# Score banks, mask products and the split of a residual in a two-block hybrid network

## The reference, cut to what matters

```
z = rmsnorm(x) @ w_in                     # cut into four mixers of 4 heads x 64
o_a = retention(q, k, v)                  # scores (k q^T) * decay, times v
o_b = gated_delta(q, k, v, beta, g)       # needs the inverse of (1 + beta * kk)
o_c, o_d = gated_linear(q, k, v, log_f)   # scores with a decay per channel
x  = x + concat(norm(o) * gates) @ w_out            # product "mix_out"
x  = x + attn(rmsnorm(x) * att_norm, mem) @ wo      # product "att_o"
x  = x + conv_ffn(rmsnorm(x) * ffn_norm)            # begins with product "up_0"
```

## Time and profile before

| | |
|---|---|
| median of the runs | 2508.35 us |
| the profiled execution | 2508.84 us, span 2507.0 us |
| PE busy | 2406.8 us, 96% of the span |
| DVE busy | 1731.7 us, 69% |
| ACT busy | 677.4 us, 27% |
| POOL busy | 196.8 us, 8% |
| granted clock of TensorE over the span | 0.98 |

### The profile page before, as it was taken

One profiled execution on the slowest core, in us unless ns is written; L12 is line 12 of the kernel. 1 busy time (PEld: TensorE's weight loads), 2 busy tenths in 40 slices (PEclk: granted clock), 3 DMA queues, 4 the chain that ended last, 5 costly groups with the idle time before them and its releaser, 6 DMA issues. The chain is left out here.

```text
span 2507.0 us, 34255 instructions
## 1 busy us (share of the span) xinstructions
PE 2406.8 (96%) x13948; PEld 1951.7 (78%) x13948; DVE 1731.7 (69%) x2700; ACT 677.4 (27%) x1248; POOL 196.8 (8%) x169
## 2 busy tenths in 40 slices
PE   8997879999999999999999999999999999999997
PEld 6885768887788888787765578888888888888886
DVE  7663666866888875738878777666666886666653
ACT  3212444012111110423577712222202112322200
POOL 0001341100000002000121010000010001000001
PEclk9998989999999999999999999999999999999999
DMA  5220002331233354422210073323463452223341
GB/s 186 76 74 0 3 19 76 111 118 51 84 96 98 97 186 146 152 68 76 76 35 1 2 247 98 109 93 101 149 239 107 160 214 72 93 93 101 122 143 63
DMA packets 70333, 252.82 MB, mean 101 GB/s; under 512 B 7808, under 2 KB 8096, under 8 KB 69664
## 3 DMA queue, kind: packets, MB, share of 16 engines
q1 hardware_dynamic: 69888, 250.08, 29.9%
q10 hardware_dynamic: 288, 0.54, 0.1%
HBM read 248.50 MB, written 2.10 MB: 100 GB/s over the span
## 5 line engine op out<-in xcount | busy, mean ns | idle before, releaser
L393 PE MATMUL psum<-rounded_n,rounded_high 128*128 128x512 f32 x1856 | 737.9, 398 | 4.4 <-DVE rounded_n_low L547 1.8
L395 PE MATMUL psum<-rounded_n,rounded_ring 128*128 128x512 f32 x1856 | 725.3, 391 | 0.0
L394 PE MATMUL psum<-rounded_n_low,rounded_high 128*128 128x512 f32 x1856 | 725.1, 391 | 0.0
L347 DVE TENSOR_TENSOR rounded_ring<-ring,rounded_high 128x1024 fp32r<-128x1024 f32 (+1 forms) x360 | 446.4, 1240 | 43.4 <-ACT rounded_high L330 31.4
L393 PEld LDWEIGHTS psum<-rounded_n,rounded_high 128*128 128x128 f32 x1856 | 350.4, 189 | 84.9 <-issue 7.5
L394 PEld LDWEIGHTS psum<-rounded_n_low,rounded_high 128*128 128x128 f32 x1856 | 350.4, 189 | 77.4 <-issue 5.5
L395 PEld LDWEIGHTS psum<-rounded_n,rounded_ring 128*128 128x128 f32 x1856 | 350.0, 189 | 73.7
L345 DVE CAST rounded_high<-ring 128x1024 fp32r<-128x1024 f32 (+1 forms) x347 | 236.6, 682 | 189.1 <-PE psum L395 182.2
L393 PE MATMUL psum<-rounded_arena,rounded_high 128*128 128x512 f32 x720 | 280.9, 390 | 4.4 <-DVE rounded_ring L347 4.4
L394 PE MATMUL psum<-rounded_arena,rounded_high 128*128 128x512 f32 x720 | 280.6, 390 | 0.0
L395 PE MATMUL psum<-rounded_arena,rounded_ring 128*128 128x512 f32 x720 | 280.6, 390 | 0.0
(11 more groups left out here) (478 smaller groups left out, 3030.4 us busy)
## 6 DMA issues: line engine op xcount, KB each, us to landing
ring<-in_w_up SPq DMA_DIRECT2D x132, 512.0 KB, 3.5
ring<-in_w_down SPq DMA_DIRECT2D x48, 512.0 KB, 3.5
n_low<-in_mod_w SPq DMA_DIRECT2D x48, 512.0 KB, 5.6
arena<-in_mod_w SPq DMA_DIRECT2D x48, 512.0 KB, 5.4
ring<-in_w_ab_in SPq DMA_DIRECT2D x37, 512.0 KB, 3.5
ring<-in_w_mix_in SPq DMA_DIRECT2D x31, 512.0 KB, 3.5
ring<-in_w_sc_in SPq DMA_DIRECT2D x24, 512.0 KB, 5.4
ring<-in_w_down SPq DMA_DIRECT2D x24, 384.0 KB, 3.1
```

The costliest lines, as they stand in the source:

```text
L347: nc.vector.tensor_tensor(self.rounded(raw), raw, self.rounded(high), ALU.subtract).then_inc(self.weights_split, 1)
L393: self.nc.tensor.matmul(out, w_high, x_high, start=first, stop=False)
L394: self.nc.tensor.matmul(out, w_high, x_low, start=False, stop=False)
L395: return self.nc.tensor.matmul(out, w_low, x_high, start=False, stop=last)
```

## The change

It consists of five edits in two functions.

1. Retention's scores alternate between two pairs of banks, G0 and G0+1 for even steps and D0+2 and D0+3 for odd ones. The wait of `ret_scores(i)` is for the weighting of step i - 2. Step 1 waits for all weighting of the delta mixer, which reads D0 to D0+3.
2. In PE's queue scores stand two steps ahead of values.
3. `first_inverse(2)` and `(3)`, which write banks D0+2 and D0+3, follow behind the last values on PE.
4. On POOL each pick stands one turn earlier: pick HEADS+x+3 ahead of the decayed keys of turn x.
5. In a residual product with a gain ACT writes the high part n from h and the gain in one activation, ahead of its square. DVE writes the low part as gain times h minus that high part in one instruction. The memory's two low parts stand ahead of it.

```diff
+    RET_BANK = (G0, D0 + 2)
...
             if i == 0:
                 pe.wait_ge(taken, TURNS)
+            elif i == 1:
+                pe.wait_ge(weighted, 2 * HEADS)
             else:
-                pe.wait_ge(ret_weighted, 2 * i)
+                pe.wait_ge(ret_weighted, 2 * i - 2)
...
         ret_scores(0)
+        ret_scores(1)
         for i in range(RETS):
             ret_values(i)
-            if i + 1 < RETS:
-                ret_scores(i + 1)
-            if i >= 2 and i % 2 == 0:
+            if i + 2 < RETS:
+                ret_scores(i + 2)
+            if i in (2, 4):
                 first_inverse(i // 2 - 1)
+        first_inverse(2)
         first_inverse(3)
...
         pick(HEADS + 1)
+        pick(HEADS + 2)
         for x in range(len(uses)):
             u, s = uses[x]
-            if HEADS + x + 2 < HEADS * len(LEVELS):
-                pick(HEADS + x + 2)
+            if HEADS + x + 3 < HEADS * len(LEVELS):
+                pick(HEADS + x + 3)
...
+            if gain is not None:
+                nc.scalar.activation(k.rounded(k.n[:, j, :]), k.h[:, j, :], ACT.Identity,
+                                     scale=gain[:, j:j + 1]).then_inc(high, 1)
...
-            if gain is not None:
-                dve.wait_ge(out, j + 1)
-                link(nc.vector.tensor_scalar(k.n_low[:, j, :], k.h[:, j, :], gain[:, j:j + 1], None,
-                                             ALU.mult))
-                split(k, link, k.n[:, j, :], k.n_low[:, j, :]).then_inc(done, 1)
             if memory is not None and 1 <= j <= 4:
                 memory.signals["low_part"](dve, 2 * j - 2)
                 memory.signals["low_part"](dve, 2 * j - 1)
+            if gain is not None:
+                dve.wait_ge(out, j + 1)
+                dve.wait_ge(high, j + 1)
+                nc.vector.scalar_tensor_tensor(k.rounded(k.n_low[:, j, :]), k.h[:, j, :], gain[:, j:j + 1],
+                                               k.rounded(k.n[:, j, :]), ALU.mult, ALU.subtract).then_inc(done, 1)
```

More of the change, by code:

```diff
@@ L1575, in ret_scores @@
                 pe.wait_ge(taken, TURNS)
+            elif i == 1:
+                pe.wait_ge(weighted, 2 * HEADS)
             else:
-                pe.wait_ge(ret_weighted, 2 * i)
+                pe.wait_ge(ret_weighted, 2 * i - 2)
             for s in range(2):
                 rows = head_rows(s)
-                last = nc.tensor.matmul(k.psum[:, G0 + s, 0:T - j * P], z[rows, RK + m, j * P:(j + 1) * P],
+                last = nc.tensor.matmul(k.psum[:, RET_BANK[i % 2] + s, 0:T - j * P], z[rows, RK + m, j * P:(j + 1) * P],
                                         z[rows, RQ + m, j * P:T], start=True, stop=True)
@@ L2037, in ret_weight @@
                 nc.vector.tensor_tensor(k.ret_w[2 * (i % 2) + s][:, 0:T - j * P],
-                                        k.psum[:, G0 + s, 0:T - j * P],
+                                        k.psum[:, RET_BANK[i % 2] + s, 0:T - j * P],
                                         k.const(f"decay{2 * m + s}")[:, 0:T - j * P], ALU.mult
@@ L2273, in residual_product @@
                                                                        "done"))
+    high = k.sem(f"{name}_high")
     squared_scaled, added_scaled = (k.sem(f"{name}_{s}_scaled") for s in ("squared", "added"))
```

## The result

The changed kernel takes 2490.29 us (2489.99 to 2491.98, 3 runs) against 2508.35: a ratio of 0.9931, 95% interval 0.9917 to 0.9945, 18.1 us faster. I forecast 2479, 29 us faster. The time is inside my range of 2467 to 2493. The direction is right and the forecast gain is 1.6 times the measured one.

The account below looks back on a forecast made before the run. TensorE, busy 96% of the span, bounds the kernel, so only its work or gaps count. Retention 11, picks 7, mix_out and mem_k 9.5 and att_o 2 sum to 29.5 us, giving a median of 2479 (range 2467 to 2493).

Parts of the forecast that it names:

- Retention: Scores ahead of values end PE's turn-taking with DVE, so the first inverse update comes 11 us earlier (5.7 to 13).
- Picks: In the inverse's steps, picks one turn earlier remove PE's 12.2 us of waits for POOL; net gain 7 us (2 to 12).
- each of the three long waits: PE's waits of 2.6 to 3.7 us for picks; each gives back 1 to 1.5 as DVE works beside POOL.
- the loop stays: Rival in the inverse's steps: POOL and DVE hinder each other, turns stay near 5 us, picks bring 2: 2484, chance 0.18.
- mix_out and mem_k: DVE's output tile falls from 5.93 to 4.7 us, mem_k's third tile starts 7.0 earlier at full clock: 9.5 us (4 to 10.5).
- POOL on the split: In mix_out POOL's sum of squares now falls on the weight tile's split and adds 0.7 us a tile (0.3 to 1.4).
- has then caught up: At mix_out's end DVE has no backlog and adds tile 7 at 463.6 instead of 469.56.
- even 5.4 is below 5.5: Argument against a remaining backlog in mix_out: DVE's upper-bound tile period of 5.4 us is still under PE's 5.5.
- att_o: At att_o's end DVE reaches tile 7 when PE does, so PE starts 2.1 us earlier; counted as 2, lower bound 0.
- the backlog stays: Rival: POOL's sum on the split costs 1.4, mem_k's wait and low clock remain, att_o gains nothing: 2487, chance 0.12.
- The other side: Rival: each of 24 earlier picks blocks DVE on the path through `take`; at 1.6 us a pick 2517, chance 0.03.
- my signs of being wrong: Turns still at 5.05, `take` ending later, DVE's mix_out period above 5.5, or DVE waiting over 0.7 for ACT's high part.

Follow-up runs that it names:

- the last kernel: Changed kernel with picks waiting for `difference`, a unit's first keys ahead, mem_k's reciprocal behind two splits, next weight tile's cast before the low part: 2478.32 us, ratio 0.9872.
- the moved ends: Changed kernel with mem_k's reciprocal behind two weight tiles' splits and the last tile's square ahead of its high part in residual products: 2491.85 us, ratio 0.9931.
- the waiting picks: Changed kernel with each step's pick waiting until its turn's `difference` is done: 2486.16 us, ratio 0.9908; together with the moved ends 2485.08 us, ratio 0.9906.

## Why the prediction was right in direction and too large

**Retention (11, measured 11.25).** The mechanism is right, and the close number is in part luck. Behind the first values the gain is 12.5 (27.4 less 14.9), near my upper bound, because the clock did not fall there. It fell earlier instead, from 218 to 225, in the key products, and the first values came 1.24 later (from the key products, 13.73 before and 14.97 now). That the second step's scores fit into PE's gap was right: PE still waits for DVE behind them, in the changed kernel and in two others:

```profile
226.42 1.08 PE L1592 MATMUL psum<-ring,n_low 128*64 128x512 f32 x4 [1.07 <-DVE ring L2043]
```
```profile
224.10 1.08 PE L1592 MATMUL psum<-ring,n_low 128*64 128x512 f32 x4 [0.72 <-DVE ring L2043]
```
```profile
225.14 1.36 PE L1589 MATMUL psum<-ring,n_low 128*64 128x512 f32 x4 [2.62 <-DVE ring L2037]
```

The second row is of the kernel without POOL's sums, with the same instructions as the changed one here. Its first values come at 13.73, as before, and its first update at 28.62, a gain of 12.5 in the stage. The third row is of the kernel with edit 5 alone, which has the old retention, and its first values come at 14.96. So the 1.24 goes with where in the key products the clock falls, and no edit decides that.

**Picks (7, measured 2 by the ratios, 1.2 to 3.7 in the traces of the stretch).** The failed step is the price of the work beside POOL: I let "each of the three long waits" give back 1 to 1.5, 3.9 in all. But nine of the 20 `difference` instructions are now blocked fully (1.75 or 1.76), where three were, so they take 1184 ns in the mean instead of 860, 6.5 us in all. Grown queries take 976 instead of 910, 1.4 more, with DVE the bound of a turn. That is 7.9 us where I had 3.9. Against the kernel with edit 4 undone, PE's waits for POOL of 12.8 us went, and those for `take` grew by 6.6 (7.1 to 13.7). My rival "the loop stays", 2 us with turns near 5, is nearest to what came: turns took 4.3 to 5.5.

Here the Trainium skill's rule (SBUF — State Buffer, section "Who interferes with whom") pointed to the right side of the term, near its lower bound. I had both it and the 1.75 us row, and priced only a part of the turns by it. The traces agree that the later one fully blocks: DVE's instructions of 0.68 and 0.69 end 0.54 to 0.56 us behind POOL's end. But not every pick cost DVE its own 1.27: DVE was busy 7.5 us more, not 24 x 1.27 = 30.

**mix_out and mem_k (9.5, measured 4.3, and at most 1.1 by the clock behind).** That PE no longer waits for splits was right: 1.7 us less to the end of mix_out, where I had 1.95. The mis-sized term is POOL on the split, 0.7 (0.3 to 1.4). It is 1.1, and at tiles without memory's parts DVE idles 0.86 for ACT where I had 0.69, so the period is 5.17 (3.9 + 0.17 + 1.1) and not 4.7. It was inside my bounds. The false step is to conclude from a period under PE's that DVE "has then caught up", and the sentence against the rival, "even 5.4 is below 5.5". Below PE's pace is not enough; the difference, 0.27 us a tile, is all that works a backlog off. 2.7 us were left at tile 7 (450.80 to 453.47), and the wait at mem_k of 2.74 and the low clock follow from them: without POOL's sums tile 7 is added on time and both are gone.

**att_o (2, measured 1.05).** The same: tile 7 is added 1.0 late. DVE's backlog, not the chain behind it, kept the rest: the last kernel has the sums and no backlog, and its pause is 3.81, near my 3.7. (The 2.73 of the kernel without sums has POOL's last addition taken out of the chain as well.)

**Rivals.** I gave each of "the loop stays" and "the backlog stays" a case of its own. Both rest on the same exclusion of DVE and POOL and came together: 11 + 2 + 4 + 0 = 17 us, 2491. The prediction has the two together only with a low clock in retention, at a chance of 0.05 and 2497. The other side (a pick at 1.6 us on the path) did not occur: even a pick that blocks fully cost DVE 1.07. Of my signs of being wrong one came, DVE's wait for ACT's high part at 0.86, above 0.7.

## What to carry to other kernels

Where VectorE bounds a loop and GpSimd works beside it in SBUF, write the SBUF-only instructions of both into one common queue and add up their times for a turn. Move GpSimd's work beside VectorE's PSUM-sourced additions, which it did not slow here: a semaphore and one changed place in GpSimd's queue took 5.6 us off a stretch of 176. A loop that is only a little faster than its partner carries a backlog to its end: price the period's difference times the number of tiles against the backlog at the start. Rivals that share a cause are one case, and their losses belong in one sum.

## What the hardware showed that I had not expected

- A cast of 128x1024 from f32 to fp32r has one input and is held by GpSimd as fully as an instruction with two: it takes 1.78 against 0.69 us, and 0.69 again when GpSimd's addition is left out.
- The same wait need not bring the same clock. Behind a wait of 1.78 before mem_k's third tile the granted clock was 0.53, and 1.00 behind one of 1.76 in another kernel with the same stage, where it did not fall in the 17 us that followed either (the first row is a window behind the wait in the kernel with the moved ends, the second in the one with the waiting picks as well):

```profile
460.00:462.00 2.00, 2.00 (x13) 2.00 (x12) 2.00 (x2) 0.00 (x0) 0.00 (x0) 0.53 0.00 0
```
```profile
456.00:458.00 2.00, 2.00 (x19) 2.00 (x18) 1.97 (x3) 0.00 (x0) 0.00 (x0) 1.00 0.28 113
```

- The same instructions take different times with edits elsewhere. The stretch of the steps takes 176.19 in the changed kernel and 179.85 in the one without POOL's sums (clock 0.95 and 0.93), and 178.60 to 179.96 in four kernels with the old picks. The stretch ahead of it takes 29.86 or 28.62, as the clock falls earlier or later in the key products. Gains of 1 to 4 us can't be read from one trace of such a stretch.
